# Attention of a second layer: products of stacked 12-bit halves in place of float32, and two elementwise steps on GpSimd

## The chip, the cores and the metric

The kernel runs on one core of a Trainium2 chip. The time is device microseconds of one execution on that core. Three runs of the kernel before gave 2525.64, 2529.07 and 2533.79 us; their median is 2529.07 us. The compute engines of the core are TensorE (PE), VectorE (DVE), ScalarE (ACT) and GpSimd (POOL); SyncE (SP) issues transfers. SBUF is the on-chip memory of 128 partitions, PSUM the eight banks that TensorE writes.

## The reference

A sequence of 512 tokens of width 1024 goes through two blocks. The first is a gated delta rule with memory attention and a gated feed-forward part. The second is a convolution module with its feed-forward part, and then the layer that the change is about: an attention in which 16 query heads share 2 groups of keys and values, each head with three branches, a bias that falls with distance (alibi), and a gate per branch. With 512 tokens the selected blocks are all blocks and the window is the whole sequence, so that the branches `slc` and `win` are two causal attentions over different keys and values. Cut to what matters:

```python
kv = (rmsnorm(h, kv_norm) @ w_kv)            # 6 parts x 2 groups x 64
k_cmp = silu((blocks_of_32(k_cmp_raw) + pos) @ w1) @ w2      # 31 compressed keys; values alike
proj = rmsnorm(x, norm_g) @ w_in             # 16 heads x 64, and 48 gates
for each branch:                             # compressed, selected, window
    s = einsum('bghqd,bgmd->bghqm', q, k) * 64 ** -0.5
    s = where(dist >= 0, s - slopes * dist, NEG)
    p = softmax(s)
    o += gates[branch] * einsum('bghqm,bgmd->bghqd', p, v)
out = o @ w_out
```

Everything is float32, and the projections `@` around it are the larger part of the work.

## The kernel before

Activations lie transposed, features on partitions and the 512 tokens in columns. A projection is made of units of 128 output features; for each unit `products` (L269) runs over 8 tiles of 128 inputs (more in the feed-forward parts). It works with 12-bit halves: a float32 value is the sum of a high part, rounded to the type fp32r, and a low part, the remainder. The weights lie in `WR` (high) and `WL` (low), the inputs in `XR`/`XL` or `MR`/`ML`, and a unit takes three products per tile, high by high, high by low and low by high (L282, L283, L284). The weights come as `raw` by DMA; their high part is made on ScalarE (L243) or GpSimd (L227), their low part always on GpSimd (L247, in `low_unit`).

The second layer's attention multiplies are not made so. They are plain float32 matmuls, one each.

**Key and value stage.** Seven units give the compressed rows, the keys and values of both branches, and the gates (`g_rows`). VectorE multiplies each by the norm `R` as it leaves PSUM (`kv_vector`, L1482, tiles counted by `tile_taken`) and, after that, the windows of the compressed rows (L1501). TensorE turns the values (L1450), runs 256 small multiplies for the compression (`phi`, L1461), two more (L1465) and turns the gates (L1469).

**Attention.** The heads go in 8 pairs (j), a pair being one head of each group (g), and each head has three branches (r): `ITEMS`, 6 items per pair and 12 per turn, 4 turns of a loop. r = 0 is the compressed branch with 32 columns per block of 128 tokens, r = 1 and 2 are the causal ones: four blocks of 512, 384, 256 and 128 columns, 1280 in all. The steps of an item n are:

- scores, `scores_tensor` L1580 (L1587 for r = 0, L1594 else);
- VectorE reads them with the alibi tile and finds the row maxima, `read_vector` L1717 (L1738; L1726, L1729 and L1731 for r = 0);
- ScalarE's exponentials with their sums, `exp_scalar` L1661 (L1676; L1666 for r = 0);
- VectorE's weights, reciprocal of the sum times the gate (L1760, L1765), and the scaling of the probabilities by them (L1775; L1770 for r = 0), `scale_vector` L1750;
- TensorE turns the scaled probabilities (`turn_probs_tensor` L1598, L1612; L1603 for r = 0), in three groups;
- the turned groups leave PSUM as `PT`, two by ScalarE (L1689) and one by VectorE (L1748);
- TensorE weighs the values into bank 7 (`weigh_tensor` L1615, L1630; L1623 for r = 0), both heads of a pair in the two halves of one bank.

After a pair, ScalarE and VectorE make the halves `MR` and `ML` of its result (L1693, L1783). The next pair's query projection (24 products into bank 0) runs behind items 1 and 7.

The order of the work is written out by hand. Each engine has its own program with a loop over the turns: TensorE does T(n), S(n+2), W(n) (turning, scores, weighing); ScalarE evicts n and then makes the exponentials of n+2; VectorE evicts n, scales n+1 and reads n+2. They meet through counting semaphores (`tile_taken`, `scored`, `probs_done`, `probs_scaled`, `turned`, ...). ScalarE also makes the two alibi tiles of each head (L1658, L1659). GpSimd makes nothing of the attention itself here, only the weight halves of the query units (8 units, L227 and L247).

## Time and profile before

| | |
|---|---|
| median of three runs | 2529.07 us (2525.64 to 2533.79) |
| the profiled execution's span | 2526.4 us, 2.7 us under that median |
| TensorE busy | 2312.5 us, 92% |
| VectorE busy | 1227.1 us, 49% |
| ScalarE busy | 939.0 us, 37% |
| GpSimd busy | 825.2 us, 33% |
| key and value stage to the first query unit | to 1795 us |
| attention, eight pairs | 1795 to 2103 us, an eighth of the span |

The span is that of the profiled execution, taken from its first to its last instruction; the runs were timed without a profile. Busy shares are of the whole span. TensorE's clock, as the throttle granted it, is given in each window as a share of full speed. Matmul durations overlap: a matmul is listed with its latency, and the distance from one start to the next is what it costs in a stream.

### The profile page before, as it was taken

To read this page: it belongs to the slowest core of one execution; us is meant where nothing else is said; L and a number is where in the kernel's file an instruction comes from. 1 tells how busy PE (TensorE), PEld (TensorE's weight loads), DVE (VectorE), ACT (ScalarE), POOL (GpSimd) and SP (SyncE) were. 2 spreads that over 40 slices of the span, in tenths; PEclk is the share of its full clock that TensorE was granted. 3 is DMA by queue.
4 is the path that set the end of the run, shared out by engine and by line. 5 is a ranking of instruction groups with operands and counts; after the bars stand their busy time and mean duration, and the time that the engine had idled before them with its cause. 6 is when DMAs were issued, how large, how long until landed. Compare 5 with 4: busy or idle time off the path is not lost.

```text
span 2526.4 us, 31399 instructions
## 1 busy us (share of the span) xinstructions
PE 2312.5 (92%) x10462; PEld 1767.5 (70%) x10462; DVE 1227.1 (49%) x1886; ACT 939.0 (37%) x1466; POOL 825.2 (33%) x366
## 2 busy tenths in 40 slices
PE   3899999998799999979869999999999999999997
PEld 2677777776578888755537888887755557788886
DVE  5466666643343332189964333325266565333322
ACT  4433343333344432241244444222144444444322
POOL 2522222221444444332204444445011102444442
PEclk8999999999889999979979999999599999999999
DMA  3211111011222232211102232422000001232322
GB/s 120 92 34 42 33 42 33 33 36 65 83 67 95 96 103 98 90 34 50 50 9 85 98 100 91 144 93 90 9 17 17 16 10 58 84 100 97 106 92 79
DMA packets 43688, 169.94 MB, mean 67 GB/s; under 512 B 4848, under 2 KB 4976, under 8 KB 43120
## 3 DMA queue, kind: packets, MB, share of 16 engines
q1 hardware_dynamic: 43056, 163.82, 19.6%
q10 hardware_dynamic: 576, 5.37, 0.5%
q8 instruction: 35, 0.57, 0.1%
q14 instruction: 21, 0.17, 0.0%
HBM read 167.08 MB, written 2.10 MB: 67 GB/s over the span
## 4 chain that ended last, share of the span: by engine, by line
PE 73%; DVE 10%; issue 9%; ACT 5%; POOL 1%; DVEq 1%; DMA 1%; ACTq 0%; POOLq 0%; SPq 0%
PE bank L282 19%; PE bank L284 19%; PE bank L283 19%; PE bank L1630 2%; PE bank L705 2%; PE bank L699 2%; ACT Pr L1676 2%; PE bank L1594 1%; PE bank L709 1%; DVE ACC L382 1%; DVE act L775 1%; PE bank L1461 1%; POOL WL L247 1%; PE bank L1612 1%; DVE Y L1364 1%
## 5 line engine op out<-in xcount | busy, mean ns | idle before, releaser
L247 POOL TENSOR_TENSOR WL<-raw,WR 128x1024 fp32r<-128x1024 f32 (+2 forms) x288 | 737.8, 2562 | 974.9 <-ACT WR L243 970.2
L282 PE MATMUL bank<-XR,WR 128*128 128x512 f32 x1528 | 631.7, 413 | 46.1 <-DVE XL L403 31.7
L284 PE MATMUL bank<-XR,WL 128*128 128x512 f32 x1528 | 603.1, 395 | 0.0
L283 PE MATMUL bank<-XL,WR 128*128 128x512 f32 x1528 | 602.7, 394 | 0.0
L243 ACT ACTIVATE WR<-raw 128x1024 fp32r<-128x1024 f32 (+2 forms) x230 | 255.7, 1114 | 743.3 <-PE bank L284 735.6
L282 PEld LDWEIGHTS bank<-XR,WR 128*128 128x128 f32 x1528 | 291.2, 191 | 124.3 <-issue 37.2
L282 PE MATMUL bank<-MR,WR 128*128 128x512 f32 (+1 forms) x856 | 336.3, 393 | 17.0 <-DVE ML L1390 7.6
L284 PEld LDWEIGHTS bank<-XR,WL 128*128 128x128 f32 x1528 | 291.3, 191 | 62.9
L283 PEld LDWEIGHTS bank<-XL,WR 128*128 128x128 f32 x1528 | 292.1, 191 | 59.8 <-issue 7.7
L283 PE MATMUL bank<-ML,WR 128*128 128x512 f32 (+1 forms) x856 | 332.7, 389 | 0.0
L284 PE MATMUL bank<-MR,WL 128*128 128x512 f32 (+1 forms) x856 | 332.3, 388 | 0.0
L227 POOL CAST WR<-raw 128x1024 fp32r<-128x1024 f32 (+1 forms) x58 | 61.0, 1052 | 675.1 <-PE bank L284 584.1
L282 PEld LDWEIGHTS bank<-MR,WR 128*128 128x128 f32 x856 | 162.9, 190 | 56.1 <-issue 14.4
L1233 DVE TENSOR_TENSOR f_up<-bank,R 128x512 f32<-128x512 f32 x66 | 45.6, 692 | 304.9 <-PE bank L284 304.9
L382 DVE TENSOR_TENSOR ACC<-ACC,SQ 128x512 f32<-128x512 f32 (+1 forms) x80 | 113.0, 1413 | 162.9 <-ACT SQ L371 161.4
L284 PEld LDWEIGHTS bank<-MR,WL 128*128 128x128 f32 x856 | 163.3, 191 | 32.8
L283 PEld LDWEIGHTS bank<-ML,WR 128*128 128x128 f32 x856 | 163.4, 191 | 31.9 <-issue 0.2
L1238 DVE TENSOR_TENSOR ML<-f_mid,MR 128x512 f32 x66 | 123.8, 1876 | 64.7 <-ACT MR L1218 64.7
L1267 PE MATMUL bank<-c_row,diag 128*128 128x512 f32 x160 | 77.9, 646 | 23.1 <-ACT diag L1313 23.1
L1188 DVE TENSOR_TENSOR hT<-bank,hT 128x512 f32 x24 | 16.6, 692 | 161.7 <-PE bank L284 161.7
L1630 PE MATMUL bank<-PT,v_tok 128*64 128x512 f32 (+3 forms) x256 | 82.3, 467 | 13.8 <-ACT PT L1689 13.3
L1676 ACT ACTIVATE Pr<-Pr,stats 128x512 f32<-128x512 f32 (+3 forms) x128 | 70.4, 551 | 65.5 <-DVE stats L1738 65.3
(268 smaller groups left out, 2667.1 us busy)
## 6 DMA issues: line engine op xcount, KB each, us to landing
raw<-w SPq DMA_DIRECT2D x224, 512.0 KB, 3.3
raw<-w SPq DMA_DIRECT2D x48, 704.0 KB, 4.0
raw<-w SPq DMA_DIRECT2D x16, 384.0 KB, 3.0
hT<-xT SPq DMA_DIRECT2D x1, 2048.0 KB, 8.0
hT<-xT ACTq DMA_DIRECT2D x1, 2048.0 KB, 7.9
phi<-phi ACTq DMA_DIRECT2D x1, 2048.0 KB, 8.8
out<-Y SPq DMA_DIRECT2D x8, 256.0 KB, 2.0
memT<-memT ACTq DMA_DIRECT2D x1, 1024.0 KB, 8.1
```

The lines of the kernel that those rows point to most:

```text
L227: nc.gpsimd.tensor_copy(WR[:, here], raw[:, here]).then_inc(high_split, 1)
L243: nc.scalar.activation(WR[:, here], raw[:, here], ACT.Identity).then_inc(high_ahead, 1)
L247: nc.gpsimd.tensor_tensor(WL[:, here], raw[:, here], WR[:, here].bitcast(F32), ALU.subtract).then_inc(weight_split, 1)
L282: nc.tensor.matmul(into, wr, xr(k0 + k), start=start, stop=False)
L283: nc.tensor.matmul(into, wr, xl(k0 + k), start=False, stop=False)
L284: mm = nc.tensor.matmul(into, wl, xr(k0 + k), start=False, stop=stop)
L382: nc.vector.tensor_tensor(ACC[:, 0:width], ACC[:, 0:width], SQ[:, parity * SEQ:parity * SEQ + width], ALU.add).then_inc(summed, 1)
L699: mm = nc.tensor.matmul(bank[4][:, here], joins[:, here], g_["U"][:, here], start=True, stop=True)
L1238: nc.vector.tensor_tensor(cols(ML, n), f_mid[:, :], cols(MR, n).bitcast(F32), ALU.subtract).then_inc(mid_low, 1)
L1267: mm = nc.tensor.matmul(bank[4 + j][:, :], diag[j][:, k * P:(k + 1) * P], c_row[j][:, 2 + k:2 + k + SEQ], start=k == 0, stop=k == PE_TAPS - 1)
L1630: mm = nc.tensor.matmul(bank[7][rows, kb * P:], v_tok[r - 1][:, kb * P + 64 * g:kb * P + 64 * g + 64], PT[:, col:col + (NB - kb) * P], sta ...
L1676: ins = nc.scalar.activation(here, here, ACT.Exp, bias=stat(idx, 0)[:, b:b + 1], scale=-1.0, accum_out=stat(idx, 1)[:, b:b + 1])
```

## The change

The attention's multiplies go over to stacked halves. The query of each head becomes `Q_S[j][g]`, 128 partitions, the high part in the 64 partitions of its group and the low part in the other 64. Keys become `KS[i][g][0]`, the high part in both halves, and `KS[i][g][1]`, the low part in both (`KC` for the compressed ones). Two products over 128 partitions then take the place of one float32 matmul over 64. The values `VS` carry high and low side by side, 64 and 64 columns, and the turned probabilities leave PSUM in two versions, `PTH` by ScalarE and `PTL`, the remainder, by VectorE: eight products for four, with 128 output rows. The two halves of the output stand above each other in a bank of their own for each head (`ACCUM`, bank 7 and bank 0) and are added by a copy on ScalarE and an addition on VectorE into `y_sum`. The low part of the result `ML` is made on GpSimd.

The scaling of the probabilities moves from VectorE to GpSimd (four operations per item), and so do the alibi tiles from ScalarE. The inputs of the query units are multiplied by `R` before their halves are made, so that the query isn't multiplied later. The query projection is made in two pieces of four tiles, one behind W(n) and one ahead of W(n+1). In the key and value stage the windows stand ahead of the `g_rows` tile, the gates are turned ahead of the last two small multiplies, and the halves of keys and values are made. The first two low parts of the weights of the output projection (`out2`) are made inside GpSimd's attention program.

The core of the diff:

```diff
 scores_tensor:
-            pe.wait_ge(tile_taken, i * 2 + (q_tiles + idx // N_ITEMS * 2 + j + 1))
+            pe.wait_ge(q_ready, half_nth(i, idx) + 1)
...
-                    mm = nc.tensor.matmul(bank[2 + n][:, at0:at0 + (b + 1) * P], qT[j][rows, b * P:(b + 1) * P],
-                                          k_rows[r - 1][rows, 0:(b + 1) * P], start=True, stop=True)
+                    for part in range(2):
+                        mm = nc.tensor.matmul(bank[2 + n][:, at0:at0 + (b + 1) * P], Q_S[j][g][:, b * P:(b + 1) * P],
+                                              KS[r - 1][g][part][:, 0:(b + 1) * P], start=part == 0, stop=part == 1)
 weigh_tensor:
-            for kb in range(NB):
-                col = KEYS_AT[kb]
-                mm = nc.tensor.matmul(bank[7][rows, kb * P:], v_tok[r - 1][:, kb * P + 64 * g:kb * P + 64 * g + 64],
-                                      PT[:, col:col + (NB - kb) * P], start=False, stop=r == 2 and kb == NB - 1)
+            for part, (ready, PT) in enumerate(((pT_high, PTH), (pT_low, PTL))):
+                for n, pieces in enumerate(TURNED):
+                    pe.wait_ge(ready, m * 3 + (n + 1))
+                    for kb, col in pieces:
+                        last = part == 1 and n == len(TURNED) - 1
+                        mm = nc.tensor.matmul(into[:, kb * P:], VS[r - 1][:, g * SEQ + kb * P:g * SEQ + (kb + 1) * P],
+                                              PT[:, col:col + (NB - kb) * P], start=False, stop=r == 2 and last)
 attend_tensor:
+                    nxt = (i, 1) if n < 6 else (i + 1, 0)
+                    if n % 6 == 1 and exists(i, n + 6):
+                        pair_tensor(pe, *nxt, DT // 2, DT)
                     weigh_tensor(pe, i, n)
-                    if n == 1:
-                        pair_tensor(pe, i, 1)
-                    if n == 7 and exists(i, N_ITEMS):
-                        pair_tensor(pe, i + 1, 0)
+                    if n % 6 == 0 and exists(i, n + 6):
+                        pair_tensor(pe, *nxt, 0, DT // 2)
 evict_scalar:
-            for n, source_bank in ((0, bank[5]), (2, bank[1])):
+            for n, ((first, end), source_bank) in enumerate(zip(GROUPS, TURN_BANKS)):
                 act.wait_ge(turned, s_nth(i, idx) * 3 + (n + 1))
-                nc.scalar.activation(PT[:, first:end], source_bank[:, 0:end - first], ACT.Identity).then_inc(pT_act, 1)
+                nc.scalar.activation(PTH[:, first:end], source_bank[:, 0:end - first], ACT.Identity).then_inc(pT_high, 1)
 evict_vector:
-                dve.wait_ge(turned, m * 3 + 2)
-                nc.vector.tensor_copy(PT[:, 512:1024], bank[6][:, :]).then_inc(pT_dve, 1)
+            for n, ((first, end), source_bank) in enumerate(zip(GROUPS, TURN_BANKS)):
+                dve.wait_ge(pT_high, s_nth(i, idx) * 3 + (n + 1))
+                V.tensor_tensor(PTL[:, first:end], source_bank[:, 0:end - first], PTH[:, first:end].bitcast(F32),
+                                ALU.subtract).then_inc(pT_low, 1)
 q_vector:
-            nc.vector.tensor_tensor(qT[j][:, :], bank[0][:, :], R[:, :], ALU.mult).then_inc(tile_taken, 1)
+            for g in range(2):
+                dve.wait_ge(q_high, i * 4 + (2 * j + g + 1))
+                nc.vector.tensor_tensor(Q_S[j][g][HALF[1 - g], :], bank[0][HALF[g], :], Q_S[j][g][HALF[g], :].bitcast(F32),
+                                        ALU.subtract).then_inc(q_ready, 1)
 new:
+        def half_scalar(act, i, j, g):
+            act.wait_ge(half_done, i * 4 + (2 * j + g + 1))
+            nc.scalar.activation(y_half[HALF[g], :], ACCUM[g][HALF[1 - g], :], ACT.Identity).then_inc(half_copied, 1)
+        def half_vector(dve, i, j, g):
+            dve.wait_ge(half_copied, i * 4 + (2 * j + g + 1))
+            nc.vector.tensor_tensor(y_sum[HALF[g], :], ACCUM[g][HALF[g], :], y_half[HALF[g], :], ALU.add).then_inc(half_summed, 1)
+        def scale_gpsimd(pool, i, idx):
+            wait_apart(pool, weight_ready, weight_mark(i, idx))
+            P_, w = Pr[s_parity(idx)], stat(idx, 3)
+            for b in (3, 2, 0, 1):
+                here = P_[:, WHERE[b]:WHERE[b] + (b + 1) * P]
+                ins = nc.gpsimd.tensor_scalar(here, here, w[:, b:b + 1], None, ALU.mult)
+            ins.then_inc(probs_scaled, 1)
```

VectorE in the middle of a turn. Before: the weights of an item, its four scalings, the reading of the next item's scores and the copy of one turned group.

```order
L1760 RECIPROCAL stats<-stats 128x4 [waits probs_done]
...
L1765 TENSOR_TENSOR stats<-stats,gates 128x4
...
L1775 TENSOR_SCALAR Pr_147<-Pr_147,stats 128x512 [waits weight_ready]
L1775 TENSOR_SCALAR Pr_147<-Pr_147,stats 128x384
L1775 TENSOR_SCALAR Pr_147<-Pr_147,stats 128x128
L1775 TENSOR_SCALAR Pr_147<-Pr_147,stats 128x256
...
L1738 ISA Pr_148,stats<-bank,alibi_140 128x512 [waits scored]
...
L1738 ISA Pr_148,stats<-bank,alibi_140 128x384 [waits scored]
...
L1738 ISA Pr_148,stats<-bank,alibi_140 128x256 [waits scored]
...
L1748 COPY PT<-bank 128x512 [waits turned]
...
L1760 RECIPROCAL stats<-stats 128x4 [waits probs_done]
```

With the change, in the same place (`PTL` is the low part of the turned probabilities, `y_sum` the sum of two output halves):

```order
L1862 RECIPROCAL stats<-stats 128x4 [waits probs_done]
...
L1866 TENSOR_TENSOR stats<-stats,gates 128x4
...
L1831 ISA Pr_157,stats<-bank,alibi_165 128x512 [waits scored]
...
L1831 ISA Pr_157,stats<-bank,alibi_165 128x384 [waits scored]
...
L1831 ISA Pr_157,stats<-bank,alibi_165 128x256 [waits scored]
...
L1879 TENSOR_TENSOR y_sum<-bank,y_half 64x512 [waits half_copied,y_low]
L1845 TENSOR_TENSOR PTL<-bank,PTH 128x512 [waits pT_high] x2
L1845 TENSOR_TENSOR PTL<-bank,PTH 128x256 [waits pT_high]
...
L1862 RECIPROCAL stats<-stats 128x4 [waits probs_done]
```

The four scalings are gone from between weights and reading, and in place of one copy stand three subtractions, each of which waits for ScalarE's copy, and an addition that waits for another.

ScalarE, before, where the exponentials of one item meet the copies of another (`Pr` are the probabilities):

```order
L1658 ACTIVATE alibi_c_141<-table,params 128x128
L1659 ACTIVATE alibi_139<-table,params 128x512
...
L1676 ACTIVATE Pr_148,stats<-Pr_148,stats 128x512 [waits piece_read]
...
L1676 ACTIVATE Pr_148,stats<-Pr_148,stats 128x384 [waits piece_read]
L1676 ACTIVATE Pr_148,stats<-Pr_148,stats 128x128
...
L1676 ACTIVATE Pr_148,stats<-Pr_148,stats 128x256 [waits scores_read]
...
L1689 ACTIVATE PT<-bank 128x512 [waits turned]
...
L1689 ACTIVATE PT<-bank 128x256 [waits turned]
```

With the change, at items 6 and 7 of a turn, the first two of its second pair (`PcS` is the compressed item's stack):

```order
L1770 ACTIVATE y_half<-bank 64x512 [waits half_done]
L1757 ACTIVATE PcS<-bank 32x512 [waits c_turned]
L1749 ACTIVATE Pr_157,stats<-Pr_157,stats 128x512 [waits piece_read]
L1749 ACTIVATE Pr_157,stats<-Pr_157,stats 128x384 [waits piece_read]
L1749 ACTIVATE Pr_157,stats<-Pr_157,stats 128x128
L1749 ACTIVATE Pr_157,stats<-Pr_157,stats 128x256 [waits scores_read]
L1761 ACTIVATE PTH<-bank 128x512 [waits turned] x2
L1761 ACTIVATE PTH<-bank 128x256 [waits turned]
```

The copies are three per item instead of two, the exponentials of the next item but one stand ahead of the second set, and a copy of an output half stands ahead of one of them; the alibi tiles are gone.

GpSimd, with the change, behind the low part of one weight unit (before, GpSimd has only the cast and the subtraction of each weight unit there):

```order
L247 TENSOR_TENSOR WL<-raw,WR 128x1024 [waits high_split]
L1917 TENSOR_TENSOR alibi_c_155<-table,params 128x128 [waits scores_read]
L1918 TENSOR_TENSOR alibi_165<-table,params 128x512
L1925 TENSOR_SCALAR Pr_156<-Pr_156,stats 128x512 [waits weight_ready]
L1925 TENSOR_SCALAR Pr_156<-Pr_156,stats 128x384
...
L1931 TENSOR_TENSOR ML<-y_sum,MR 128x512 [waits y_high]
L1925 TENSOR_SCALAR Pr_157<-Pr_157,stats 128x512 [waits weight_ready]
...
L1925 TENSOR_SCALAR Pr_157<-Pr_157,stats 128x256
L1917 TENSOR_TENSOR alibi_c_154<-table,params 128x128 [waits scores_read]
L1918 TENSOR_TENSOR alibi_164<-table,params 128x512
L1954 CAST WR<-raw 128x1024 [waits weight_loaded1,unit_done]
L1925 TENSOR_SCALAR Pr_156<-Pr_156,stats 128x512 [waits weight_ready]
```

Scalings, the result's low part, alibi tiles and the weight units now stand in one queue, each behind its own wait.

## Rows read from the trace of the kernel before

**Rows 1.** The page: its head, and the chain that ended last by engine.

```profile
span 2526.4 us, 31399 instructions
...
PE 73%; DVE 10%; issue 9%; ACT 5%; POOL 1%; DVEq 1%; DMA 1%; ACTq 0%; POOLq 0%; SPq 0%
```

**Rows 2.** Windows: length, busy us of PE, PEld, DVE, ACT, POOL; granted clock; DMA share, GB/s.

```profile
1795.00:1843.00 48.00, 44.51 (x153) 27.50 (x154) 20.67 (x71) 14.84 (x41) 6.77 (x4) 0.75 0.07 22
1843.00:1992.00 149.00, 140.78 (x637) 85.05 (x636) 90.10 (x320) 68.48 (x204) 13.56 (x8) 0.99 0.04 14
```

**Rows 3.** Timeline of TensorE, one pair of heads: start, duration, engine, line, operation, idle before.

```profile
1922.63 2.42 PE L1594 MATMUL bank<-k_rows,qT 64*128 64x512 f32 x8
1924.98 2.37 PE L1630 MATMUL bank<-PT,v_tok 128*64 128x512 f32 x8
1927.28 0.61 PE L1603 MATMUL bank<-table,Pc 128*32 128x128 f32 x4
...
1930.17 1.07 PE L1623 MATMUL bank<-PcT,v_cmp 32*64 32x512 f32 x2
...
1936.75 0.50 PE L282 MATMUL bank<-MR,WR 128*128 128x512 f32 x1
...
1942.32 1.25 PE L1612 MATMUL bank<-table,Pr 128*128 128x128 f32 x10
...
1963.43 0.61 PE L1603 MATMUL bank<-table,Pc 128*32 128x128 f32 x4
```

**Rows 4.** Timeline of TensorE, products of 256 columns in layer 1.

```profile
67.07 0.28 PE L283 MATMUL bank<-ML,WR 128*128 128x256 f32 x1
67.19 0.28 PE L284 MATMUL bank<-MR,WL 128*128 128x256 f32 x1
```

**Rows 5.** Timeline of VectorE in the attention.

```profile
1918.85 1.27 DVE L1775 TENSOR_SCALAR Pr<-Pr,stats 128x512 f32<-128x512 f32 x4
...
1923.12 0.28 DVE L1758 TENSOR_REDUCE stats<-Pc 128x4 f32<-128x128 f32 x1
...
1924.42 0.69 DVE L1738 CUSTOM_DVE_ANT_0 Pr<-bank,alibi 128x512 f32<-128x512 f32 x1
...
1928.33 0.69 DVE L1783 TENSOR_TENSOR ML<-bank,MR 128x512 f32 x1 [2.18 <-ACT MR L1693]
1928.94 0.17 DVE L1760 RECIPROCAL stats<-stats 128x4 f32<-128x4 f32 x1
...
1929.44 0.81 DVE L1775 TENSOR_SCALAR Pr<-Pr,stats 128x512 f32<-128x512 f32 x2
```

**Rows 6.** Timeline of ScalarE in the attention.

```profile
1922.08 1.04 ACT L1689 ACTIVATE PT<-bank 128x512 f32<-128x512 f32 x2 [0.77 <-PE bank L1612]
1925.15 0.72 ACT L1676 ACTIVATE Pr<-Pr,stats 128x512 f32<-128x512 f32 x1 [2.04 <-DVE stats L1738]
...
1927.26 0.18 ACT L1676 ACTIVATION_READ_ACCUMULATOR Pr<-Pr,stats 128x1 f32 x1
```

**Rows 7.** GpSimd's groups by line and form: count, busy us, mean ns, idle before.

```profile
L247 POOL TENSOR_TENSOR WL<-raw,WR 128x1024 fp32r<-128x1024 f32 x224 | 553.8, 2473 | 711.7 <-ACT WR L243 707.2
...
L227 POOL CAST WR<-raw 128x1024 fp32r<-128x1024 f32 x56 | 59.4, 1061 | 655.6 <-PE bank L284 573.4 <-issue 68.7 <-DMA raw<-w 13.5
...
L227 POOL CAST WR<-raw 128x768 fp32r<-128x768 f32 x2 | 1.6, 824 | 19.5 <-PE bank L284 10.7 <-issue 8.8
```

**Rows 8.** Timelines of GpSimd and VectorE at the attention's start; L1731's shortest, median, longest.

```profile
1804.03 2.34 POOL L247 TENSOR_TENSOR WL<-raw,WR 128x1024 fp32r<-128x1024 f32 x1
...
1805.36 1.16 DVE L1731 TENSOR_TENSOR Pc<-Pc,c_max 128x128 f32<-128x128 f32 x1
...
L1731 DVE TENSOR_TENSOR Pc<-Pc,c_max x16: 291/291/1159, 1805.4 to 2083.4; 128x128 f32<-128x128 f32 x16
```

**Rows 9.** Timeline of TensorE in the key and value stage.

```profile
1765.74 26.28 PE L1461 MATMUL bank<-windows,phi 64*64 64x32 f32 x256 [4.58 <-DVE windows L1501]
...
1795.35 0.79 PE L282 MATMUL bank<-MR,WR 128*128 128x512 f32 x1 [0.45 <-DVE gates L1510]
```

More of the change, by code:

```diff
@@ L1523, in program @@
         TURNED = [[(0, 0)], [(1, 512), (3, 896)], [(2, 1024)]]
-        KEYS_AT = {kb: col for piece in TURNED for kb, col in piece}
+        TURN_BANKS = (bank[5], bank[6], bank[1])
         KEY_SCALE = 0.125
@@ new lines, in program @@
+        PTL = at("PTL", 177 * KB, PCOLS, F32R)
+        PcS = at("PcS", 182 * KB, SEQ, F32R, parts=64)
+        alibi_c = [at(f"alibi_c{g}", 184 * KB + 512 * g, P) for g in range(2)]
+        Pr = [at(f"Pr{m}", (32 + 5 * m) * KB, PCOLS) for m in range(2)]
+        PTH = at("PTH", 42 * KB, PCOLS, F32R)
+        Pc = at("Pc", 47 * KB, P)
+        stats = at("stats", 47 * KB + 512, 48)
+        c_max = at("c_max", 47 * KB + 704, 8)
+        y_half = at("y_half", behind_r, SEQ)
+        y_sum = at("y_sum", behind_r + 2 * KB, SEQ)
@@ L1605, in turn_probs_tensor @@
                 return
+            pe.wait_ge(probs_scaled, s_nth(i, idx) + 1)
             P_ = Pr[s_parity(idx)]
-            for pieces, (first, _), into in zip(TURNED, GROUPS, (bank[5], bank[6], bank[1])):
+            for pieces, (first, _), into in zip(TURNED, GROUPS, TURN_BANKS):
                 for kb, col in pieces:
```

296 lines of the change are left out of this document (202 added, 94 removed).

## The prediction

> **What bounds the kernel now.** I read the page first: the chain that ended last is 73% TensorE [rows 1]. The windows of the attention say the same: from 1843 to 1992 us TensorE is busy 140.8 of 149 us, VectorE 90 and ScalarE 68, at a granted clock of 0.99, and from 1795 to 1843 us the clock is 0.75 [rows 2]. The timeline of TensorE gives the period. One pair of heads runs from its L1603 at 1927.28 to the next at 1963.43: **36.15 us** [rows 3]. In it stand four score groups (step 2.35 us each, L1594), four weighings (2.30, L1630), transposes (1.25, L1612, and 0.55, L1603), two compressed weighings (1.0, L1623), two compressed scores of about 1.0 and one projection of 5.57 (24 products from 1936.75 to 1942.32) [rows 3]: 9.4 + 9.2 + 5.0 + 1.1 + 2.0 + 2.0 + 5.6 = 34.3 us. Only 1.9 us of a pair is idle: TensorE is the bound, and float32 multiplies are 22.6 us of it.
>
> **What the change takes from TensorE.** An fp32r product costs a step of 0.12 us at 256 columns [rows 4] and 5.57/24 = 0.23 at 512 [rows 3]. For 384 I take 0.17. No row shows 128 columns: below, proportion gives 0.06, above, the 512 step 0.23; I take 0.11, near the row at 256. A piece set (512, 384, 256, 128) twice is 2 x (0.23 + 0.17 + 0.12 + 0.11) = 1.26 us, for scores and for weighing. A compressed weighing falls from two products to one on the two halves stacked, 0.42 with its start; the compressed scores, as many products as before of another kind, stay at 1.0 at most. TensorE's work becomes 4 x 1.26 + 4 x 1.26 + 0.8 + 2.0 + 5.0 + 1.1 + 5.6 = **24.6 us per pair**, 9.7 less than now.
>
> **What the change adds around it.** A wait chain closes between three engines whose programs keep their order. VectorE does for item n its low parts L(n) (L1845), then the weights C(n+1) (L1862, L1866), then the score read D(n+2) (L1831). ScalarE does E(n), the high parts (L1761), then X(n+2), the exponentials (L1749), so E(n) stands behind X(n+1), which waits for D(n+1), which stands behind L(n-1). GpSimd does P(n), the scaling, after C(n); TensorE's transposes T(n) wait for P(n). The durations, from rows of before:
> - T to the first group ready 0.66, the first copy out 0.6 (two take 1.04 with a 256 one behind, L1689) [rows 6], then three subtractions on VectorE. One of bank and MR in 512 columns steps 0.61 [rows 5]; 0.62 + 0.62 + 0.42 = 1.66. From T's start to L's end: 3.0 us.
> - C: 0.5 (1928.94 to 1929.44); 1.3 for the compressed branch (1923.12 to 1924.42). D: first piece 0.7 [rows 5]. X: 2.29 (1925.15 to 1927.44) [rows 6].
> - P: four operations of 512, 384, 256, 128 columns, so far 1.27 us on VectorE (L1775) [rows 5], now on GpSimd. No row has this operation there. Its cast gives (1061 - 824)/256 = 0.93 ns a column and 0.11 fixed: 1280 columns and four starts are 1.65 us. Its two-input subtraction takes 2473/1024 = 2.4 ns a column: 3.1 us [rows 7]. These are my ends on the slow side; VectorE's 1.27 is the quick one. I take 1.65, since a scaling reads one tile as the cast does, and 0.1 for each hand-over.
>
> The Trainium skill, "GPSIMD Engine Reference", section Engine selection, speaks against this move: elementwise work belongs on VectorE, GpSimd being about 2x slower with two inputs and roughly at line rate with one. The L227 and L247 rows agree with both halves of it. By line rate, P would be the 1.27 of L1775 and the sum 4 us less.
>
> **The period after.** From the end of L to the end of the next L:
> - Items 1 and 2 (n%6) carry the next pair's projection in two halves and stay TensorE's: 0.42 + 2.9 + 1.24 + 1.0 + 2.9 + 1.3 + 0.1 + 3.0 = 12.9.
> - The two low halves of the query on VectorE: 1.24.
> - Item 3 (compressed): C 1.3, D 0.73, X 2.29, half copy 0.6 (L1770), E 0.57, L 0.7: 6.2.
> - Item 4: 0.5 + 0.73 + 2.29 + 0.6 + 1.66 and hops: 5.8.
> - Item 5, by way of GpSimd: 0.5 + 0.1 + 1.65 + 0.1 + 3.0 = 5.4.
> - Item 0: as item 3, 6.3, and 0.4 for a VectorE operation that stands behind GpSimd's `low_unit` or alibi tile. Before shows such a case: L1731, 291 ns in the median, took 1.16 us while L247 ran from 1804.03 [rows 8]; once in two pairs that is 0.4.
>
> Sum **38.2 us against 36.15**, +2.1. For seven pairs that is 14.7. The eighth has no projection to do: before it would have been 36.15 - 5.57 = 30.6, after, items 1 and 2 fall back to their loop of 5.4 to 5.8 each and the query's 1.24 goes, 35.2: +4.6. The attention gets 19.3 us longer at full clock.
>
> The Trainium skill, "SBUF — State Buffer", section Who interferes with whom, calls this an exclusive lock: a VectorE operation with two SBUF inputs waits out a GpSimd operation that reads SBUF, one with a PSUM input doesn't. The L1731 row agrees; the many subtractions of the change read PSUM, so by it they stay free, and the sum is as it stands. Were they held as well, with the 0.87 us that L1731 lost there once in each item, a pair would get 5.2 us longer and the result 2592.
>
> **The other parts.** Moving P and the alibi tiles off VectorE and ScalarE saves nothing, since they weren't the bound. GpSimd's own load is 4 x 1.65 + 1.2 (L1931) + 3.1 (alibi) + 1.0 + 2.4 = 14.4 of 38, at no cost by itself; what queues behind a wait there is priced in item 0. The key and value stage: the windows (L1501) no longer stand behind the `g_rows` tile. L1461 had waited 4.58 us for them [rows 9]; it now waits for the seventh tile, some 2.4 us sooner. The gate transposes leave the end of the stage, where the first projection waited for the gates copy [rows 9]: about 2 sooner. Together -4.5. The added copies of keys and values (16 operations) lie beside 26 us of L1461: nothing; if that cover is too short, up to +4. The first query fill adds 0.65 (two copies and two lows for one multiply). out2 waits for the last half sums: 1.3. q_scale and q_low double VectorE's operations under the kv units, about 6.2 us against 5.4 us a unit, caught up later: 0, at most +4.
>
> **The clock.** From 1795 to 1843 us the grant is 0.75 [rows 2], after TensorE had run the 64-column multiplies of L1461. The engine has two levels, 1.2 and 2.4 GHz, and this mean loses (1 - 0.75) x 48 = 12 us of granted time already. After the change TensorE idles a third of the time, and no row of before shows how the grant follows that. Ends: nothing, and all that TensorE has on the path (some 13 us a pair, items 1 and 2) at the lower level, +13 a pair. I take +4, a third of one pair at that level: the attention's own row from 1843 us is the nearest, with 0.99, and it is the start of the stage, behind L1461, where the level can come later than now.
>
> Sum: 19.3 + 0.65 - 4.5 + 1.3 + 4 = +20.8. The profiled execution's span is 2526.4, 2.7 below the median of the runs: 2526.4 + 20.8 + 2.7 = **2550 us**.
>
> **The rivals.**
> - *GpSimd scales at the two-input rate.* P is 3.1, 1.45 more. Item 5 gets it whole; item 4 goes by way of P, 0.5 + 0.1 + 3.1 + 0.1 + 3.0 = 6.8, 1.0 more; and in items 0 to 2, where P stands behind GpSimd's `low_unit`, alibi tiles and L1931, the backlog costs about 3. In all 5.4 a pair: 2550 + 43 = 2593. For it: the operation carries a pointer to a scalar per partition. Against: it reads one tile only. Chance 0.12.
> - *TensorE stays the bound, and the kernel is faster.* The place is L(n-1) to L(n) in items 3, 4, 5 and 0. If that loop took less than TensorE's own 4.1 us an item (24.6/6), a pair would take 4 x 1.9 = 7.6 less than my 38.2: 30.6, and the result is 2550 - 61 = 2489. It decides at a mean of 5.5 an item instead of my 6.0 (8 x 4 x 0.5 = 16 us). For it: 10 us of TensorE's work are really gone. Against: X and the subtractions are measured, and their order is fixed. Chance 0.16.
> - *Both cancel.* Loops shorter by some 0.5 each, or P at 1.27 with the full clock kept: 2530. Chance 0.14.
> - *The multiplies don't get cheap.* Should fp32r at 128 columns cost the full 0.23, TensorE's work grows by 16 x 0.12 = 1.9 a pair, still below 36. Only items 1 and 2 see it, 0.5 a pair: +4. This is inside the forecast.
>
> **How the numbers follow.** My forecast, the loops with P near 1.65, has 0.58. About 0.3%, 7.6 us, is what a measurement of this kernel can tell from no change. Slower: 0.58 + 0.12 = 0.70; same 0.14; faster 0.16. The range goes from 2522, which leaves out the faster rival, to 2592, which takes in the clock's end in part and stops at the slow scaling: about 0.13 of the one and 0.06 of the other lie outside.
>
> **What the profile after would show.** Right: TensorE busy some 65 to 70% in the attention instead of 94%; the compressed transposes of one pair and the next 38 to 39.5 us apart; VectorE's idle time ended by ScalarE's PTH (L1761), ScalarE's by VectorE's stats (L1831), TensorE's by L1845 and GpSimd's L1925; L1925 at about 0.4 us on average; L1461 starting 2.4 us earlier against the last unit. Wrong: TensorE still busy over 90% (faster rival); L1925 near 0.78 on average (slow scaling); a granted clock well under 0.9 from 1843 us on (my clock term is too small); VectorE's L1845 at much over 0.69 for 512 columns (the lock reaches them).

## The result, and the profile after

The changed kernel takes **2615.14 us** in the median (2613.38 to 2616.32, 4 runs), the kernel before beside it 2528.64. The ratio is 1.0341 with an interval of 1.0327 to 1.0356: slower, as forecast, by 86.5 us and not by 21, and outside the range of 2522 to 2592.

The page of the changed kernel (first its head, then busy time by engine, then the granted clock in 40 slices):

```profile
span 2614.5 us, 31623 instructions
...
PE 2293.1 (88%) x10446; PEld 1825.5 (70%) x10446; DVE 1255.8 (48%) x1874; ACT 967.7 (37%) x1514; POOL 994.7 (38%) x534
...
PEclk8999999999799999799899999996777678999999
```

Its window over the middle of the attention, columns as in [rows 2]:

```profile
1843.00:1992.00 149.00, 106.31 (x485) 90.71 (x486) 73.60 (x230) 59.28 (x163) 73.98 (x70) 0.73 0.03 11
```

TensorE is busy 106 of 149 us (71%) where it was 94%; the forecast had 65 to 70%. Its clock is granted at 0.73 where it was 0.99, and that wasn't forecast. VectorE fell from 90 to 74 us and ScalarE from 68 to 59: nobody is full, so a chain of waits is the bound. TensorE's timeline shows which, over one pair, from one L1675 to the next but one:

```profile
1905.28 0.60 PE L1675 MATMUL bank<-table,Pc 128*32 128x128 f32 x4
...
1923.31 1.31 PE L1685 MATMUL bank<-table,Pr 128*128 128x128 f32 x10 [2.51 <-POOL Pr L1925]
...
1938.95 2.39 PE L1685 MATMUL bank<-table,Pr 128*128 128x128 f32 x10 [4.43 <-POOL Pr L1925]
...
1947.52 2.40 PE L1685 MATMUL bank<-table,Pr 128*128 128x128 f32 x10 [2.12 <-POOL Pr L1925]
...
1953.24 0.60 PE L1675 MATMUL bank<-table,Pc 128*32 128x128 f32 x4
```

The pair is now 1953.24 - 1905.28 = **47.96 us** against 36.15 [rows 3]. Ahead of three of the four turnings of a pair (L1685; items 2, 4 and 5) TensorE stands 2.1 to 4.4 us for `Pr`, and what ends it is GpSimd's L1925. Item 1's turning waits for nothing: it stands behind the first half of the projection. Where the clock is low, the turning itself takes 2.39 us in place of 1.31. GpSimd's groups by line and form:

```profile
L1925 POOL TENSOR_SCALAR Pr<-Pr,stats 128x512 f32<-128x512 f32 x32 | 50.0, 1563 | 178.4 <-DVE stats L1866 178.4
L1925 POOL TENSOR_SCALAR Pr<-Pr,stats 128x384 f32<-128x384 f32 x32 | 39.8, 1243 | 0.0
L1925 POOL TENSOR_SCALAR Pr<-Pr,stats 128x256 f32<-128x256 f32 x32 | 29.5, 922 | 0.0
L1925 POOL TENSOR_SCALAR Pr<-Pr,stats 128x128 f32<-128x128 f32 x32 | 19.3, 602 | 0.0
...
L1918 POOL TENSOR_TENSOR alibi<-table,params 128x512 f32<-128x512 f32 x16 | 16.7, 1042 | 0.0
```

Four scalings are 1563 + 1243 + 922 + 602 ns = **4.33 us** an item, where the prediction took 1.65, had 3.1 as its slow end, and VectorE had needed 1.27 [rows 5]. VectorE's timeline gives the items, from the end of one set of low parts to the end of the next (start plus duration; L1845 of a causal item, L1841 of a compressed one, L1807 the query):

```profile
1902.04 1.02 DVE L1845 TENSOR_TENSOR PTL<-bank,PTH 128x512 fp32r<-128x512 f32 x2 [0.16 <-ACT PTH L1761]
...
1908.84 0.68 DVE L1841 TENSOR_TENSOR PcS<-bank,PcS 32x512 fp32r<-32x512 f32 x1 [0.19 <-issue]
...
1924.63 1.62 DVE L1845 TENSOR_TENSOR PTL<-bank,PTH 128x512 fp32r<-128x512 f32 x3 [4.81 <-ACT PTH L1761]
...
1926.28 1.41 DVE L1807 TENSOR_TENSOR QS<-bank,QS 64x512 fp32r<-64x512 f32 x2
...
1933.24 0.68 DVE L1841 TENSOR_TENSOR PcS<-bank,PcS 32x512 fp32r<-32x512 f32 x1 [2.42 <-ACT PcS L1757]
...
1941.59 1.02 DVE L1845 TENSOR_TENSOR PTL<-bank,PTH 128x512 fp32r<-128x512 f32 x2 [0.16 <-ACT PTH L1761]
...
1950.15 1.02 DVE L1845 TENSOR_TENSOR PTL<-bank,PTH 128x512 fp32r<-128x512 f32 x2 [0.16 <-ACT PTH L1761]
```

| item of the pair | forecast, us | measured | from, to |
|---|---|---|---|
| 0 | 6.7 | 6.5 | 1903.06 to 1909.52 |
| 1 and 2 | 12.9 | 16.7 | to 1926.25 |
| query | 1.2 | 1.4 | to 1927.69 |
| 3 | 6.2 | 6.2 | to 1933.92 |
| 4 | 5.8 | 8.7 | to 1942.61 |
| 5 | 5.4 | 8.6 | to 1951.17 |
| sum | 38.2 | 48.1 | |

Where no scaling by GpSimd is on the path (0, 3, the query) the forecast holds to 0.2 us. The missing 9.9 us lie in the four causal items. The 3.8 of items 1 and 2 aren't all the scaling's: the projection's first half, 12 products in item 1, took 4.54 us (from 1910.05 to 1914.59) where the prediction had 2.9, at a granted clock of 0.63.

The key and value stage moved little. In the changed kernel everything from L387 on is 2.83 us later, for a reason that lies ahead of all changed code and stays open. In the kernel before:

```profile
1726.58 1.02 PE L387 MATMUL bank<-ACC,table 128*128 128x512 f32 x2
```

In the changed kernel (TensorE's L387, L1478 and first query product; VectorE's first windows, L1545, and its `g_rows` tile, L1548):

```profile
1729.41 1.02 PE L387 MATMUL bank<-ACC,table 128*128 128x512 f32 x2
...
1759.52 3.61 DVE L1545 TENSOR_TENSOR windows<-c_rows,params 128x496 f32<-128x496 f32 x2
...
1768.08 0.67 DVE L1548 COPY g_rows<-bank 48x512 f32<-48x512 f32 x1
...
1769.01 1.25 PE L1478 MATMUL bank<-windows,phi 64*64 64x32 f32 x10 [5.01 <-DVE g_rows L1548]
...
1796.94 0.80 PE L282 MATMUL bank<-MR,WR 128*128 128x512 f32 x1
```

From L387, L1461 started at 1765.74 - 1726.58 = 39.16 us and its successor L1478 starts at 39.60; the first query product came at 68.77 and comes at 67.53. So the stage gave back 1.2 us, not 4.5. The first windows were in fact ready sooner, at 1759.52 + 3.61 = 1763.13, 33.7 us behind L387. But the changed kernel's TensorE waits ahead of L1478 for the `g_rows` tile as well, and VectorE makes that behind all the windows: it ends at 1768.75, 39.3 us behind L387, and L1478 starts 0.26 later. From the first query product to the first of `out2` it was 307.3 us, and is 395.4: **+88.1 us, all of the loss, lies in the attention**.

### The profile page after: what moved, and what is told of

The parts are those of the page before. It is cut to its first block, busy times and chain, and to the rows that moved or that the text cites. A ratio compares the mean times of both kernels' runs of the same rounds, so it can differ in the third digit from the quotient of the medians.

```text
span 2614.5 us, 31623 instructions
## 1 busy us (share of the span) xinstructions
PE 2293.1 (88%) x10446; PEld 1825.5 (70%) x10446; DVE 1255.8 (48%) x1874; ACT 967.7 (37%) x1514; POOL 994.7 (38%) x534
## 4 chain that ended last, share of the span: by engine, by line
PE 69%; DVE 11%; issue 10%; ACT 5%; POOL 4%; DVEq 1%; DMA 0%; POOLq 0%; ACTq 0%; SPq 0%
PE bank L282 19%; PE bank L284 18%; PE bank L283 18%; POOL Pr L1925 3%; PE bank L705 2%; PE bank L1685 2%; PE bank L699 2%; PE bank L709 1%; DVE ACC L382 1%; DVE act L775 1%; ACT Pr L1749 1%; PE bank L1478 1%; DVE PTL L1845 1%; POOL WL L247 1%; DVE Y L1364 1%
## 5 line engine op out<-in xcount | busy, mean ns | idle before, releaser
L247 POOL TENSOR_TENSOR WL<-raw,WR 128x1024 fp32r<-128x1024 f32 (+2 forms) x288 | 738.7, 2566 | 926.1 <-ACT WR L243 922.1
L282 PE MATMUL bank<-XR,WR 128*128 128x512 f32 x1528 | 632.3, 414 | 46.2 <-DVE XL L403 31.7
L282 PEld LDWEIGHTS bank<-XR,WR 128*128 128x128 f32 x1528 | 291.0, 190 | 124.5 <-issue 37.5
L282 PE MATMUL bank<-MR,WR 128*128 128x512 f32 (+1 forms) x856 | 342.3, 400 | 17.3 <-DVE ML L1390 7.6
L283 PE MATMUL bank<-ML,WR 128*128 128x512 f32 (+1 forms) x856 | 338.1, 395 | 0.0
L284 PE MATMUL bank<-MR,WL 128*128 128x512 f32 (+1 forms) x856 | 337.8, 395 | 0.0
L227 POOL CAST WR<-raw 128x1024 fp32r<-128x1024 f32 (+1 forms) x50 | 53.5, 1070 | 410.4 <-PE bank L284 380.8
L282 PEld LDWEIGHTS bank<-MR,WR 128*128 128x128 f32 x856 | 166.2, 194 | 57.6 <-issue 14.7
L1925 POOL TENSOR_SCALAR Pr<-Pr,stats 128x512 f32<-128x512 f32 (+3 forms) x128 | 136.4, 1083 | 178.4 <-DVE stats L1866 178.4
L284 PEld LDWEIGHTS bank<-MR,WL 128*128 128x128 f32 x856 | 166.8, 195 | 33.7
L1685 PE MATMUL bank<-table,Pr 128*128 128x128 f32 x320 | 62.3, 365 | 77.9 <-POOL Pr L1925 77.9
L1845 DVE TENSOR_TENSOR PTL<-bank,PTH 128x512 fp32r<-128x512 f32 (+1 forms) x96 | 53.6, 598 | 148.8 <-ACT PTH L1761 148.8
L1685 PEld LDWEIGHTS bank<-table,Pr 128*128 128x128 f32 x320 | 51.2, 188 | 88.0 <-POOL Pr L1925 88.0
```

Source lines behind the costliest of these rows:

```text
L227: nc.gpsimd.tensor_copy(WR[:, here], raw[:, here]).then_inc(high_split, 1)
L247: nc.gpsimd.tensor_tensor(WL[:, here], raw[:, here], WR[:, here].bitcast(F32), ALU.subtract).then_inc(weight_split, 1)
L282: nc.tensor.matmul(into, wr, xr(k0 + k), start=start, stop=False)
L283: nc.tensor.matmul(into, wr, xl(k0 + k), start=False, stop=False)
L284: mm = nc.tensor.matmul(into, wl, xr(k0 + k), start=False, stop=stop)
L1685: mm = nc.tensor.transpose(into[:, at0:at0 + P], P_[:, c:c + P], ident)
```

## The experiments

Each kernel was timed beside the kernel before on the same chip; ratios are to that one. e1 to e4 and e12 start from the changed kernel; e5 to e9 and e11 take parts of the change back, and e10 is the kernel before with one alteration.

### e1 and e3: the scaling back on VectorE; e2: the scaling in another form on GpSimd

```diff
 scale_vector (e1, e3):
+            dve.wait_ge(weight_ready, weight_mark(i, idx))
+            P_ = Pr[s_parity(idx)]
+            for b in (3, 2, 0, 1):
+                here = P_[:, WHERE[b]:WHERE[b] + (b + 1) * P]
+                ins = V.tensor_scalar(here, here, w[:, b:b + 1], None, ALU.mult)
+            ins.then_inc(probs_scaled, 1)
 attend_gpsimd (e1, e3): the four scale_gpsimd calls of a pair go
 scale_gpsimd (e2):
-                ins = nc.gpsimd.tensor_scalar(here, here, w[:, b:b + 1], None, ALU.mult)
+                ins = nc.gpsimd.tensor_tensor(here, here, w[:, b:b + 1].broadcast_to([P, (b + 1) * P]), ALU.mult)
```

> The four scalings of an item go back from GpSimd to VectorE, behind the weights and ahead of the next read; all else as in the changed kernel. The changed kernel has them at 4.3 us an item (1.56 + 1.24 + 0.92 + 0.60) against the 1.27 they took on VectorE. Theory A (this price is the lost time): items 4 and 5 of a pair fall from 8.7 and 8.6 to about 7.1 (the loop by way of the exponentials, now 1.27 longer) and 5.3, items 1 and 2 from 16.7 to about 13.7; the pair from 48.0 to about 40 us, the kernel to about 2553 (2545 to 2565). Theory B (the lower clock is most of it, and would stay): 2590 or more.

> The scalings stay on GpSimd, but each is a tensor_tensor with the weight's column broadcast, the form of the alibi tiles (L1917, L1918: 0.40 us at 128 columns, 1.04 at 512), in place of tensor_scalar. Theory A: by those two rows an item's four cost 4 x 0.19 + 1280 x 1.67 ns = 2.9 us instead of 4.3; three to four of them on a pair's path, 4.2 to 5.6 us a pair, 2575 (2567 to 2585). Theory C (GpSimd's price is set by the two SBUF reads of the tile in place, whatever the form): unchanged, 2615.

> As e1, and the alibi tiles back on ScalarE where the kernel before had them: what is left of the change is the attention's multiplies and their copies. Theory A: against e1 the VectorE operations that stood behind a GpSimd operation (0.4 a pair) are free, ScalarE has 1.1 us more ahead of the exponentials of one item per head; 2550 (2544 to 2562). Rival: ScalarE's place in the loop is full, and the two tiles come whole, 2.2 us a pair, 2570.

Measured: e1 2573.68 us (ratio 1.0177, 1.016 to 1.0194), e2 2576.42 (1.018, 1.0163 to 1.0197), e3 2571.78 (1.017, 1.0153 to 1.0187). All three take some 40 us back. In e2, where the form of the scaling is all that differs, the granted clock in the window from 1843 us is 0.74, as low as the changed kernel's 0.73 (e1 0.77, e3 0.82): those 38.7 us are not the clock's. GpSimd's two ends in e2:

```profile
L1925 POOL TENSOR_TENSOR Pr<-Pr,stats 128x512 f32<-128x512 f32 x32 | 33.3, 1040 | 178.3 <-DVE stats L1866 178.3
...
L1925 POOL TENSOR_TENSOR Pr<-Pr,stats 128x128 f32<-128x128 f32 x32 | 12.7, 397 | 0.0
```

The sum of four is 2.90 us, as worked out from the alibi rows, and the time came out at the expected 2575. e1 stayed 20 us above its expected 2553, and e3 above its 2550. The second cause is seen in e3's timelines of GpSimd (L1946, L247) and VectorE (L1886):

```profile
1903.13 1.04 POOL L1946 CAST WR<-raw 128x1024 fp32r<-128x1024 f32 x1
...
1904.25 2.40 POOL L247 TENSOR_TENSOR WL<-raw,WR 128x1024 fp32r<-128x1024 f32 x1
...
1903.25 4.08 DVE L1886 TENSOR_SCALAR Pr<-Pr,stats 128x512 f32<-128x512 f32 x4
```

The four scalings that take 1.27 us elsewhere take 4.08 beside GpSimd's cast and subtraction of the next weights, once a pair. The alibi tiles' place (e3 against e1) is worth nothing measurable: e3 came out at the 2570 of its rival, but not by that rival's way, which would have put it 18 us above e1.

### e7: GpSimd's weights at another moment

```diff
 attend_gpsimd of e3:
                     wait_apart(pool, unit_done, unit - 1)
+                    wait_apart(pool, scores_read, nth(i, n + 3) + 2)
                     nc.gpsimd.tensor_copy(WR[:, here], raw[:, here]).then_inc(high_split, 1)
```

> e3 with one thing changed: GpSimd's cast and low part of the next query weights wait until VectorE has read the scores of item 3 of the pair, so that they run beside the subtractions out of PSUM and no longer beside the scaling. In e3 VectorE's L1886 takes 4.08 us instead of 1.27 in item 2, and L1875 0.99 instead of 0.17, while the cast and L247 run. If GpSimd holding VectorE is the cause: -3.5 us a pair at most, 2544 to 2552. If the 4.08 is only a long span beside something else: unchanged, 2572.

Measured: 2554.65 us (1.01, 1.0083 to 1.0117), 17 less than e3, and just outside the expected 2544 to 2552. VectorE's scalings in e7, shortest, median and longest:

```profile
L1886 DVE TENSOR_SCALAR Pr<-Pr,stats x128: 278/381/490, 1814.0 to 2124.6; 128x512 f32<-128x512 f32 x32, 128x384 f32<-128x384 f32 x32, 128x128 f32<-128x128 f32 x32, 128x256 f32<-128x256 f32 x32
```

In e3 the longest was 2516 ns. The hold is real and cost 17 us; I had put it at 28 at most.

### e4: TensorE kept busy

```diff
 turn_probs_tensor:
+            if idx % 6 != 1:
+                for _ in range(8):
+                    nc.tensor.matmul(bank[5][:, :], KS[0][0][0][:, 0:P], KS[0][0][0][:, :], start=True, stop=True)
             pe.wait_ge(probs_scaled, s_nth(i, idx) + 1)
```

> The changed kernel, with 8 added fp32r products of 512 columns on TensorE ahead of each wait for GpSimd's scaling except that of item 1 of a pair; their result is overwritten by the transposes. They need 1.9 us at full clock, in a wait that lasts 2.1 to 4.4. This only keeps TensorE busy. Theory A: what the wait for GpSimd costs stays, what the lower clock costs (transposes 2.4 for 1.3 us in items 4 and 5, the projection's first half 4.5 for 2.8) goes in part: 2590 to 2610, with a granted clock above 0.73 in the attention. Theory B (the clock is most of it): 2560 or less.

Measured: 2612.23 us (1.0326, 1.0308 to 1.0343), just outside the 2590 to 2610 of theory A, and far from B. The window, then one pair: the projection's first half and a turning on TensorE, the low parts of items 4 and 5 on VectorE (item 3's end at 1933.53):

```profile
1843.00:1992.00 149.00, 115.40 (x567) 92.82 (x564) 73.13 (x230) 58.94 (x163) 75.65 (x71) 0.85 0.03 11
...
1909.08 0.79 PE L282 MATMUL bank<-MR,WR 128*128 128x512 f32 x1
...
1914.24 1.26 PE L1688 MATMUL bank<-table,Pr 128*128 128x128 f32 x10
...
1938.58 1.31 PE L1688 MATMUL bank<-table,Pr 128*128 128x128 f32 x10 [0.46 <-POOL Pr L1928]
...
1939.90 1.62 DVE L1848 TENSOR_TENSOR PTL<-bank,PTH 128x512 fp32r<-128x512 f32 x3 [3.41 <-ACT PTH L1764]
...
1947.76 1.62 DVE L1848 TENSOR_TENSOR PTL<-bank,PTH 128x512 fp32r<-128x512 f32 x3 [4.81 <-ACT PTH L1764]
```

The granted clock rose from 0.73 to 0.85 and brought 3 us. Items 4 and 5, whose turnings now take 1.31 us, fell from 8.7 and 8.6 to 8.0 and 7.9. That is what the prediction's own path gives with the measured price, 0.5 + 0.1 + 4.33 + 0.1 + 3.0 = 8.0. Item 1 rose from 8.0 to 8.9. It has no added products; its projection half, 1909.08 to 1914.24, took 5.16 us for 4.54, at a granted clock of 0.52. So the run shows that at full clock items 4 and 5 still take 8 us by way of GpSimd, and that the low clock costs them 0.7 us each. It doesn't price the clock as a whole, since the projection kept the low one.

### e12: what is left when the scaling costs what the prediction took

This kernel leaves three of an item's four scalings out.

```diff
 scale_gpsimd:
-            for b in (3, 2, 0, 1):
+            for b in (3,):
```

> The changed kernel with three of the four scalings of an item left out (the blocks of 384, 256 and 128 columns stay unscaled), so that GpSimd's share is the one of 512 columns, 1.56 us, near the 1.65 that the prediction took for all four. All else, the clock's behaviour included, is as in the changed kernel. Theory A (the scaling's price is all that the sum lacked): the prediction's own number, 2550 (2540 to 2558). By a straight line through the changed kernel (4.33 us, 2615) and the broadcast form (2.90 us, 2576): 2576 - 1.34 x 27 = 2540. Theory B (the clock term was missed as well, and doesn't hang on the price): 2565 or more.

Measured: 2557.19 us (1.0112, 1.0095 to 1.0129), at the upper edge of A. Its pair, in it the first half of the projection (from L282 to L1685), the same half in the first pair, where the clock was high, and its window:

```profile
1813.47 0.50 PE L282 MATMUL bank<-MR,WR 128*128 128x512 f32 x1
...
1816.33 1.25 PE L1685 MATMUL bank<-table,Pr 128*128 128x128 f32 x10
...
1887.52 0.61 PE L1675 MATMUL bank<-table,Pc 128*32 128x128 f32 x4
...
1893.53 0.79 PE L282 MATMUL bank<-MR,WR 128*128 128x512 f32 x1
...
1898.64 1.25 PE L1685 MATMUL bank<-table,Pr 128*128 128x128 f32 x10
...
1928.70 0.61 PE L1675 MATMUL bank<-table,Pc 128*32 128x128 f32 x4
...
1843.00:1992.00 149.00, 119.87 (x571) 101.45 (x569) 86.06 (x267) 68.90 (x190) 49.32 (x42) 0.77 0.04 14
```

The pair is 41.18 us against the forecast's 38.2. Items 3, 4 and 0 are 7.7 with the query, 6.0 and 6.5 (forecast 7.4, 5.8, 6.7), items 1 and 2 are 14.9 (12.9) and item 5 is 6.2 (5.4). In item 1 the projection's first half takes 5.11 us, and 2.86 in the first pair: the 2.0 us of items 1 and 2 are the lower clock's. Most of the **3.0 us a pair** over the forecast is so the clock's price with a fast scaling; this is read from the trace, and no run changed the clock alone.

### e5, e6, e8: half of the change each

e5 keeps the stacked halves for the scores and takes the weighing back to float32; e6 is the mirror. Both have the scaling on VectorE and the alibi tiles on ScalarE. In e5 the projection is undivided and the result comes out of bank 7 as before the change.

```diff
 e5, weigh_tensor and evict_scalar as before the change:
+            pe.wait_ge(pT_low, m + 1)
+            pe.wait_ge(pT_high, m * 2 + 2)
+            for kb in range(NB):
+                col = KEYS_AT[kb]
+                mm = nc.tensor.matmul(bank[7][rows, kb * P:], v_tok[r - 1][:, kb * P + 64 * g:kb * P + 64 * g + 64],
+                                      PT[:, col:col + (NB - kb) * P], start=False, stop=r == 2 and kb == NB - 1)
 e6, scores_tensor as before the change:
+                    mm = nc.tensor.matmul(bank[2 + n][:, at0:at0 + (b + 1) * P], qT[j][rows, b * P:(b + 1) * P],
+                                          k_rows[r - 1][rows, 0:(b + 1) * P], start=True, stop=True)
 e8, attend_gpsimd of e5: the cast where it was, and ahead of low_unit
+                    wait_apart(pool, c_scaled, c_nth(i, n + 3) + 1)
```

> Only the scores take stacked halves. The weighing is float32 again (one product per block, one set of copies out of PSUM, both heads into bank 7), scaling on VectorE, alibi tiles on ScalarE, the projection undivided, the weight units in GpSimd's plain loop. Theory A (the loop of the changed kernel closes through the second set of copies, not through the scores): TensorE's work is 34.3 - 4 x 1.1 = 29.9 us a pair with the 1.9 idle of before, 31.8 for 36.15; 8 x -4.35 = -35: 2495 (2485 to 2512), faster than before. Rival D (the loop of reading and exponentials, 0.7 + 2.3 + 1.8 an item, binds as soon as TensorE gives way): no faster than 2525.

> The mirror of e5: only the weighing takes stacked halves, scores are float32 products of 64 rows; otherwise as e3 (scaling on VectorE, alibi tiles on ScalarE). Theory A: the loop of e3 stays whole, the query's two copies and two subtractions (1.4 on a pair's path) go, the float32 scores add 1.1 in items 1 and 2: 2565 to 2580, as slow as e3's 2572, although 4.4 us of TensorE's work a pair come back. Rival: the scores' halves carry half of the loss, 2550.

> e5 with GpSimd's low part of the query weights held until the compressed probabilities of item 3 are scaled. If in e5 as well a scaling stands behind GpSimd: 1 to 3 us a pair faster than e5 (8 to 24). If before's accident holds there, in which no scaling was ever behind GpSimd (L1775 at most 0.49): the same as e5 within 4 us.

Measured: e5 2526.52 us (0.9992, 0.9983 to 1.0002), e6 2581.43 (1.0202, 1.0185 to 1.0219), just above the expected 2565 to 2580, and e8 2527.75 (0.9997, 0.9987 to 1.0007). The loss belongs to the weighing's side and not to the scores. That its part is the second set of copies out of PSUM is argued and not shown: e5 also takes back the output halves and the divided projection. And e5 brought no gain either, against my expectation of 2495 and in line with rival D. TensorE's waits in e5's attention (total us, times, longest us):

```profile
PE bank L1679 <- ACT PT L1741: 13.4, 13, 2.5
PE bank L1661 <- DVE Pr L1842: 6.2, 14, 0.7
PE bank L1672 <- DVE ML L1850: 5.0, 7, 0.8
```

TensorE now stands for ScalarE's copies, which stand behind exponentials, and for the scaling. In e8 nothing was to be had, since no scaling in e5 stood behind GpSimd either (at most 489 ns).

### e9, e10, e11: one item more lead

The same arithmetic, with scores made and read three items ahead, the probabilities in four buffers, and the alibi tiles one item earlier.

```diff
 e9 (on e5), e10 (on the kernel before), e11 (on e7, with e11's wait moved to item n + 4):
-            return sum(1 for it in ITEMS[:idx % N_ITEMS] if it[2]) % 2
+            return sum(1 for it in ITEMS[:idx % N_ITEMS] if it[2]) % 4
...
-                    if exists(i, n + 2):
-                        scores_tensor(pe, i, n + 2)
+                    if exists(i, n + 3):
+                        scores_tensor(pe, i, n + 3)
...
-                    if exists(i, n + 2):
-                        read_vector(dve, i, n + 2)
+                    if exists(i, n + 3):
+                        read_vector(dve, i, n + 3)
...
-            if item(idx)[2] == 2 and exists(i, idx + 1):
-                alibi_scalar(act, i, idx + 1)
+            if item(idx)[2] == 1 and exists(i, idx + 2):
+                alibi_scalar(act, i, idx + 2)
```

> e5 (only the scores in stacked halves) with scores made and read three items ahead instead of two, in four buffers for the probabilities instead of two, and the alibi tiles one item earlier; no arithmetic changes. In e5 a read waited behind the weights and the scaling of the item before, these for its exponentials, and these for its read: 0.7 + 2.3 + 1.8 = 4.8 us an item, as much as TensorE's 4.8. Theory F (that loop ate e5's gain): it opens, the pair falls to TensorE's 29.9 and about 1.5 idle, 8 x 4.7 = 38 less than before: 2492 to 2505. Rival G (the granted clock eats it: TensorE idles a little and runs low for it): 2515 to 2527.

> The kernel before with the same deeper lead and nothing else. It shows what the lead is worth where TensorE is the bound. TensorE has 34.3 of 36.15 us a pair: 15 us at most. Theory F: most of the idle 1.9 goes, 2517 to 2523. Rival: its waits are for copies out of PSUM, which the lead does not touch: 2527 to 2530.

> e7 (the change's multiplies whole, scaling on VectorE, alibi tiles on ScalarE, GpSimd's weight work held back) with the same deeper lead. E(n) then no longer stands behind exponentials that wait for VectorE. Theory F: items 3, 4, 5, 0, now 7.7, 6.9, 5.5, 6.3, fall to VectorE's own 5.4 (1.95 read, 0.5, 1.27, 1.66) or less, the pair from 41 to about 34: 2500 to 2520. Rival G (clock and VectorE): 2535 or more.

Measured: e9 **2490.93 us** (0.9848, 0.9833 to 0.9863), e10 2551.61 (1.0092, 1.0076 to 1.0108), e11 2507.48 (0.9916, 0.9902 to 0.9929). e9 beats both kernels, by 1.5% and 4.7%. Its pair and its windows:

```profile
1876.95 0.61 PE L1651 MATMUL bank<-table,Pc 128*32 128x128 f32 x4
...
1910.24 0.61 PE L1651 MATMUL bank<-table,Pc 128*32 128x128 f32 x4
...
1843.00:1992.00 149.00, 140.72 (x715) 98.31 (x714) 96.37 (x355) 79.69 (x232) 16.22 (x10) 0.98 0.04 14
```

This pair is 33.29 us for 36.15 and the next is 31.64; the two kinds alternate. TensorE is at 94% and the clock at 0.98, and the total is 1 us under the range of theory F. Only the lead, with its buffers and the earlier alibi tiles, separates e5 from e9. So the order of the work held e5, and the 35.6 us are what that cost together with the clock, which was 0.93 in e5's window. e11 has the change's multiplies whole, and the same lead took 47 us off e7. Its pair:

```profile
1912.43 0.61 PE L1675 MATMUL bank<-table,Pc 128*32 128x128 f32 x4
...
1946.74 0.61 PE L1675 MATMUL bank<-table,Pc 128*32 128x128 f32 x4
```

34.31 us, as expected. So the whole change, with the scaling back on VectorE, GpSimd's weight work moved and the deeper lead, is 0.8% faster than the kernel before.

e10 went against my expectation, with 22 us more than the kernel before. In a pair without disturbance it does what was expected, 35.12 us for 36.15 (last two rows). But at the end of a turn VectorE stands 3.7 and then 1.8 us with "issue", that is with nothing in the profile that it waited for; TensorE then waits 6.18 us, and runs at the lower clock until about 1912 us (granted 0.50 from 1896, 0.98 from 1912):

```profile
1896.88 0.18 DVE L1761 RECIPROCAL stats<-stats 128x4 f32<-128x4 f32 x1 [3.73 <-issue]
...
1900.53 2.39 PE L1612 MATMUL bank<-table,Pr 128*128 128x128 f32 x10 [6.18 <-DVE Pr L1776]
...
1937.74 0.61 PE L1603 MATMUL bank<-table,Pc 128*32 128x128 f32 x4
...
1972.86 0.61 PE L1603 MATMUL bank<-table,Pc 128*32 128x128 f32 x4
```

The pair with it (1891.42 to 1937.74) takes 46.3 us, 11 more than the undisturbed ones and 10 more than before. VectorE has a second such pause a turn later, in a pair of 46.5 us. The two make most of the loss. The first L1603 also comes 3.6 us later (1814.68 for 1811.04), with one more group of scores ahead of it. Why VectorE pauses there in e10 and not in e9 wasn't tried and stays open.

## Why the prediction was wrong

**The direction, and the mechanism, were right.** TensorE's work fell as worked out (at full clock a weighing of e12, from L1706 at 1903.38 to the next turning at 1904.64, is the 1.26 us taken), the kernel became a loop through VectorE, ScalarE and GpSimd, and that loop is longer than what it replaced. Items 0 and 3 came out to 0.2 us. The direction doesn't hang on the wrong price: e7, with the scaling at VectorE's 1.27 us, is still 1% slower than the kernel before.

**The step that failed is the price of GpSimd's scaling: "I take 1.65, since a scaling reads one tile as the cast does."** It is 4.33. The scaling by a column of weights has (1563 - 602)/384 = 2.50 ns a column and 0.28 us fixed. The cast's 0.93 ns, from which the 1.65 came, is far from that. The two-input subtraction's 2.4 is near, but the slow end of 3.1 took no fixed part for four operations. So the two rows didn't bound the price. e1, e2 and e12 show the price as the cause in three ways: 4.33 us gives 2615, 2.90 gives 2576, 1.56 gives 2557. The first two differ by 1.43 us an item and 38.7 us, 3.4 items of a pair; the next 1.34 us bring 19.2, 1.8 items of a pair. With the price near the 1.65 taken, 58 of the 65 us that the forecast missed are gone.

The rival "GpSimd scales at the two-input rate" named the right mechanism with 0.12 and 2593; with the measured 4.33 in place of its 3.1, its own working gives 2.68 more in item 5 and 2.2 in item 4, 8.0 us each as in e4, and the backlog in 1 and 2.

**The clock term, +4 us, was too small.** With the price out of the way (e12) a pair is 3.0 us over the forecast, most of it by the low clock, where I took 4 us for all eight pairs. I had called it nearer the low end because of the window at 0.99, in which TensorE had no waits to speak of; no window of before showed an attention with 2 to 4 us of waiting in each item, and the changed kernel's is granted 0.73. That e12 still came out only 7 us above the forecast is luck in part: I had compared with before's quickest pairs. Its first seven took 264.0 us (L1603 from 1811.04 to 2075.07) and not seven times 36.15, 253.1; the first alone was 42.3 us, with TensorE the bound at the low clock, and is 36.6 in e12.

**The key and value stage gave 1.2 us, not 4.5.** I had L1461's successor wait "for the seventh tile, some 2.4 us sooner". That tile is `g_rows`, and by the change it stands in VectorE's order behind the windows, so that L1478 started 0.4 us later against L387 and not 2.4 sooner. VectorE has no gap over 0.2 us from 1733.14 to 1768.75: the added scalings and low parts of the inputs fill it, some of them held beside GpSimd (L1522, 0.75 us elsewhere, took 2.77 at 1748.58 beside L247). From L1478 to the first query product it is 27.9 us for 29.6: that is the gate transposes' part, 1.7 for the 2 taken. This is read from the trace and wasn't tried alone.

**The hold between GpSimd and VectorE** was priced at 0.4 us a pair, in item 0. It came in item 2: there L1866, with two small inputs in SBUF and 0.17 us elsewhere, took 1.01 us at 1917.76, and about that once in every pair, ahead of the weights that GpSimd's scaling waits for. The many subtractions out of PSUM stayed at 690 ns for 512 columns, so that half of the rule of the Trainium skill ("SBUF — State Buffer", section Who interferes with whom) agrees. The same section names `tensor_scalar` among the VectorE operations that can contend with GpSimd, which I left out: e3's 4.08 for 1.27 us agrees with it, and e7 took 17 us back. It means that moving the scaling to GpSimd had something for it, and cost more than it saved.

**The advice against the move** in the Trainium skill ("GPSIMD Engine Reference", section Engine selection) was right, and its figure of roughly line rate for one input doesn't hold for this form: 4.33 us against VectorE's 1.27 is 3.4 times. And 1.27 for my 1.65 would have taken 8 x 0.38 = 3 us off the sum, not 4.

**My expectation for e5** repeated the error in small: it took work off TensorE with "the 1.9 idle of before" and didn't ask whether the loop behind it, 4.8 us an item by rows that I had, was as long as TensorE's 4.8.
